# Output projection's last three tiles and the up projection's first three, in token halves

## The reference, cut to what matters

```python
def rmsnorm_2(x, g):
    y = xf * lax.rsqrt(jnp.mean(xf * xf, axis=-1, keepdims=True) + EPS)
    return (y * g.astype(jnp.float32)).astype(x.dtype)
...
    o = jnp.einsum('bhtm,bmhd->bthd', p, v).reshape(B, T, D_MODEL)
    return o @ w_o                      # cross attention's output projection
...
def conv_glu_ffn(h, w_up, conv_w, conv_b, w_down):
    u = causal_dwconv(h @ w_up, conv_w) + conv_b
    a, b = jnp.split(u, 2, axis=-1)
    return (jax.nn.silu(a) * b) @ w_down
```

## Time and profile before

| | |
|---|---|
| median of the timed runs | 2122.86 us |
| lowest, highest of three | 2119.52, 2123.41 us |
| profiled execution | 2120.05 us |
| span of its trace | 2118.2 us |
| TensorE busy | 2035.4 us (96%) |
| VectorE, ScalarE, GpSimd busy | 948.6, 892.0, 909.7 us |

### The profile page before, as it was taken

One profiled execution on the slowest core, in us unless ns is written; L12 is line 12 of the kernel. 1 busy time (PEld: TensorE's weight loads), 2 busy tenths in 40 slices (PEclk: granted clock), 3 DMA queues, 4 the chain that ended last, 5 costly groups with the idle time before them and its releaser, 6 DMA issues.

```text
span 2118.2 us, 27695 instructions
## 1 busy us (share of the span) xinstructions
PE 2035.4 (96%) x9940; PEld 1679.1 (79%) x9940; DVE 948.6 (45%) x1168; ACT 892.0 (42%) x1093; POOL 909.7 (43%) x419
## 2 busy tenths in 40 slices
PE   2999999999999999999999999999999989999998
PEld 2778877878787878888888878778798778888887
DVE  6155441454545453611112345877572257555313
ACT  2366663232323233333322346678554335444321
POOL 4422223434343433354444445759266133444443
PEclk9999999999999999999999999999999999999999
DMA  7221212433333322233233322220144122333331
GB/s 282 81 65 56 60 31 89 164 115 129 114 129 118 134 99 90 70 109 97 93 97 100 109 82 88 80 70 2 60 130 140 50 80 80 99 99 99 92 107 60
DMA packets 57390, 203.76 MB, mean 96 GB/s; under 512 B 6368, under 2 KB 8544, under 8 KB 57056
## 3 DMA queue, kind: packets, MB, share of 16 engines
q1 hardware_dynamic: 57312, 202.70, 29.9%
HBM read 200.57 MB, written 2.10 MB: 96 GB/s over the span
## 4 chain that ended last, share of the span: by engine, by line
PE 75%; issue 8%; DVE 7%; ACT 6%; POOL 4%; DMA 1%; POOLq 0%; DVEq 0%; SPq 0%; ACTq 0%
PE acc L1987 17%; PE acc L1989 17%; PE acc L1988 17%; PE aux L1987 5%; PE aux L1988 4%; PE aux L1989 4%; POOL w_lo L493 3%; ACT sp L552 2%; PE acc L2205 2%; PE aux L2465 1%; DVE qkvf L1660 1%; PE aux L2119 1%; DMA ada<-in_ada 1%; POOL cfy L516 1%; PE aux L2195 1%
## 5 line engine op out<-in xcount | busy, mean ns | idle before, releaser
L493 POOL TENSOR_TENSOR w_lo<-raw,w_hi 128x1024 fp32r<-128x1024 f32 x321 | 780.9, 2437 | 1137.4 <-ACT w_hi L552 1136.5
L552 ACT ACTIVATE w_hi<-raw 128x1024 fp32r<-128x1024 f32 x321 | 339.9, 1061 | 569.9 <-PE acc L1989 422.2
L1987 PE MATMUL acc<-x_hi,w_hi 128*128 128x512 f32 (+1 forms) x1336 | 526.2, 394 | 7.6 <-DVE x_lo L1531 4.1
L1988 PE MATMUL acc<-x_lo,w_hi 128*128 128x512 f32 (+1 forms) x1336 | 518.2, 388 | 0.0
L1989 PE MATMUL acc<-x_hi,w_lo 128*128 128x512 f32 (+1 forms) x1336 | 518.1, 388 | 0.0
L1987 PEld LDWEIGHTS acc<-x_hi,w_hi 128*128 128x128 f32 x1336 | 252.3, 189 | 64.4 <-issue 7.7
L1989 PEld LDWEIGHTS acc<-x_hi,w_lo 128*128 128x128 f32 x1336 | 252.0, 189 | 51.8
L1988 PEld LDWEIGHTS acc<-x_lo,w_hi 128*128 128x128 f32 x1336 | 252.3, 189 | 49.7 <-issue 0.5
L1165 DVE SCALAR_TENSOR_TENSOR adac<-ada,c_act,adac 128x1024 f32<-128x1024 f32 x42 | 65.7, 1565 | 98.2 <-DMA ada<-in_ada 97.3
L1432 DVE TENSOR_TENSOR ht<-acc,tn 128x512 f32<-128x512 f32 x21 | 14.5, 692 | 173.8 <-PE acc L1989 171.3
L1987 PE MATMUL aux<-w_hi,x_hi 128*128 128x512 f32 x192 | 75.9, 395 | 6.5 <-DVE x_lo L1193 5.2
(11 more groups left out here) (480 smaller groups left out, 3621.4 us busy)
## 6 DMA issues: line engine op xcount, KB each, us to landing
raw<-in_weights SPq DMA_DIRECT2D x324, 512.0 KB, 3.6
ada<-in_ada SPq DMA_DIRECT2D x48, 512.0 KB, 3.7
resid<-in_x SPq DMA_DIRECT2D x1, 2048.0 KB, 12.4
out<-resid SPq DMA_DIRECT2D x16, 128.0 KB, 1.7
decay<-in_tables SPq DMA_DIRECT2D x4, 256.0 KB, 3.6
memf<-in_mem SPq DMA_DIRECT2D x1, 1024.0 KB, 4.9
angles<-in_tables SPq DMA_DIRECT2D x1, 512.0 KB, 3.8
small<-in_small SPq DMA_DIRECT2D x1, 320.0 KB, 3.1
```

The lines of the kernel that those rows point to most:

```text
L493: nc.gpsimd.tensor_tensor(w_lo[s][:], raw[s][:], w_hi[s][:].bitcast(F32), ALU.subtract).then_inc(lo_ready, 1)
L552: return nc.scalar.activation(out, in_, func, **kw)
L1987: M(out, a_hi, b_hi, start=first, stop=False)
L1988: M(out, a_hi, b_lo, start=False, stop=False)
```

## The change

The last three tiles of the output projection (5, 6, 7) are computed in token halves: first all three over tokens 0 to 255, then all three over tokens 256 to 511. Each half has its own sum of squares, its own statistic of two products with a matrix of ones, and its own norm by Ln and Exp on ACT (`half_root`). The residual, x_hi and x_lo are made for the first half of the tokens and then for the second. The up projection's tiles 0 to 2 follow in halves; tile 3 stays in full width and goes with the second half. The second half of tile 5 has to be taken by DVE before TensorE may write tile 7's (`bank_free`). ACT's splits of up units 0 to 3, which stood right behind the tiles that gave back their buffers, now stand between the x_hi of the first half. The squares for norm 4 are made in full width beside the second half. The diff:

```diff
--- before.py
+++ after.py
@@ -361,6 +361,14 @@
             return bank(At(T0["down"] + n - 1)) if n else aux[:, 2 * T:3 * T]
 
         last_y = [down_bank(KT - 1)[:, HALVES[0]], aux[:, 0:T][:, HALVES[1]]]
+
+        xo_rs = [rs[:, HALVES[0]], aux[:, 3 * T:4 * T][:, HALVES[1]]]
+
+        def xo_half(n, h):
+
+            if h == 0:
+                return bank(At(T0["xo"] + n - 4))[:, HALVES[0]]
+            return (aux[:, 2 * T:3 * T][:, HALVES[0]], aux[:, 3 * T:4 * T][:, HALVES[0]], aux[:, 2 * T:3 * T][:, HALVES[1]])[n - 5]
 
         def up_bank(n):
 
@@ -1053,14 +1061,37 @@
             values_hi(2)
             turned(3)
             values_hi(3)
-            for n in range(1, 8):
+            for n in range(1, 5):
                 split_hi(At(U0["xo"] + n + AHEAD))
-            last_square(bank(At(T0["xo"] + 3)), U0["xo"] + 8)
-            split_hi(At(U0["up"] + AHEAD))
-            root(1.0 / D)
+
+            def half_square(h):
+                if h:
+                    act.wait_ge(unit_used, U0["xo"] + 8)
+                else:
+                    own["tile_done"].next(3)
+                own["last_sq"].own(f(sqt[:, HALVES[h]], xo_half(KT - 1, h), ACT.Square))
+
+            def half_root(h):
+                own["stat_ready"].next()
+                roots(xo_rs[h], 1.0 / D, xo_rs[h], own["rs_ready"])
+
+            def half_hi(k, c):
+                own["res_ready"].next()
+                own["norm_hi"].own(f(x_hi[:, k, c], resid[:, k, c], scale=norm_g[4][:, k:k + 1]))
+
+            half_square(0)
+            half_root(0)
+            split_hi(At(U0["up"]))
             for k in range(KT):
-                own["res_ready"].next()
-                own["norm_hi"].own(f(x_hi[:, k, :], resid[:, k, :], scale=norm_g[4][:, k:k + 1]))
+                half_hi(k, HALVES[0])
+                if k in (0, 2):
+                    split_hi(At(U0["up"] + k // 2 + 1))
+                if k == 4:
+                    half_square(1)
+                    split_hi(At(U0["up"] + 3))
+            half_root(1)
+            for k in range(KT):
+                half_hi(k, HALVES[1])
                 own["rsq_ready"].own(f(yv_o[:, k, :], resid[:, k, :], ACT.Square))
             split_hi(At(U0["up"] + 4))
             split_hi(At(U0["up"] + 5))
@@ -1523,26 +1554,52 @@
 
             def up_residual():
 
-                own["rs_ready"].next()
                 added = aux[:, 4 * T:5 * T]
 
-                def low(k):
+                def low(k, c):
                     own["norm_hi"].next()
-                    own["x_ready"].own(V.scalar_tensor_tensor(x_lo[:, k, :], resid[:, k, :], norm_g[4][:, k:k + 1],
-                                                              x_hi[:, k, :].bitcast(F32), ALU.mult, ALU.subtract))
+                    own["x_ready"].own(V.scalar_tensor_tensor(x_lo[:, k, c], resid[:, k, c], norm_g[4][:, k:k + 1],
+                                                              x_hi[:, k, c].bitcast(F32), ALU.mult, ALU.subtract))
 
                 def add_square(k):
                     own["rsq_ready"].next(2 if k == 1 else 1)
                     step.own(V.tensor_tensor(sqacc[:], sqacc[:] if k > 1 else yv_o[:, 0, :], yv_o[:, k, :], ALU.add))
 
+                def sublayer(k, h):
+                    c = HALVES[h]
+                    step.own(V.scalar_tensor_tensor(added[:, c], yv_o[:, k, c], norm_g[3][:, k:k + 1], xo_rs[h],
+                                                    ALU.mult, ALU.mult))
+                    own["res_ready"].own(V.tensor_tensor(resid[:, k, c], resid[:, k, c], added[:, c], ALU.add))
+
+                own["rs_ready"].next()
+                sublayer(0, 0)
+                half_tile(5, 1)
+                V.sem_inc(S["bank_free"], 1)
+                sublayer(1, 0)
+                low(0, HALVES[0])
+                sublayer(2, 0)
+                low(1, HALVES[0])
+                half_tile(6, 1)
+                sublayer(3, 0)
+                low(2, HALVES[0])
+                sublayer(4, 0)
+                low(3, HALVES[0])
+                sublayer(5, 0)
+                half_tile(7, 1)
+                low(4, HALVES[0])
+                sublayer(6, 0)
+                low(5, HALVES[0])
+                sublayer(7, 0)
+                low(6, HALVES[0])
+                low(7, HALVES[0])
+                own["rs_ready"].next()
                 for k in range(KT):
-                    step.own(V.scalar_tensor_tensor(added, yv_o[:, k, :], norm_g[3][:, k:k + 1], rs, ALU.mult, ALU.mult))
-                    own["res_ready"].own(V.tensor_tensor(resid[:, k, :], resid[:, k, :], added, ALU.add))
+                    sublayer(k, 1)
                     if k:
-                        low(k - 1)
+                        low(k - 1, HALVES[1])
                     if k in (3, 5, 7):
                         add_square(k // 2)
-                low(KT - 1)
+                low(KT - 1, HALVES[1])
                 for k in range(4, KT):
                     add_square(k)
                 V.sem_inc(S["sq_ready"], 1)
@@ -1889,15 +1946,34 @@
             normalize(3)
             out_low(2)
             out_low(3)
-            for n in range(KT):
-                if n < KT - 1:
+            def half_tile(n, h):
+
+                c, src = HALVES[h], xo_half(n, h)
+                if n == KT - 1:
+                    own["last_sq"].next()
+                    step.own(V.tensor_copy(yv_o[:, n, c], src))
+                    return
+                if h:
                     dve.wait_ge(unit_used, U0["xo"] + n + 1)
+                else:
+                    own["tile_done"].next()
+                step.own(V.tensor_copy(yv_o[:, n, c], src))
+                step.own(V.tensor_tensor(squares[:, c], src, yv_o[:, n, c], ALU.mult))
+                step.own(V.tensor_tensor(sqacc[:, c], sqacc[:, c], squares[:, c], ALU.add))
+                if n == KT - 2:
+                    V.sem_inc(S["sq_ready"], 1)
+                    own["sq_ready"].skip()
+
+            for n in range(5):
+                dve.wait_ge(unit_used, U0["xo"] + n + 1)
                 if n < 4:
                     sublayer_tile(n, aux[:, n * T:(n + 1) * T], yv_o[:, n, :], squares)
                 else:
-                    t = At(T0["xo"] + n - 4)
-                    sublayer_tile(n, bank(t), yv_o[:, n, :], squares, t)
-            invert()
+                    sublayer_tile(n, bank(At(T0["xo"])), yv_o[:, n, :], squares, At(T0["xo"]))
+            for n in range(5, KT):
+                half_tile(n, 0)
+                free(At(T0["xo"] + n - 4))
+            own["tile_done"].skip()
             up_residual()
 
 
@@ -2722,25 +2798,50 @@
             project(1, 6, 8)
             project(2, 4, 8)
             project(3, 4, 8)
-            for n in range(4, KT):
-                tile(At(U0["xo"] + n), At(T0["xo"] + n - 4), xo_hi, xo_lo)
-            two_part_stat()
-            spread_rs()
-
-            def up_part(n, first, end):
+            tile(At(U0["xo"] + 4), At(T0["xo"]), xo_hi, xo_lo)
+
+            def xo_stat(h):
+
+                c = HALVES[h]
+                own["sq_ready"].next()
+                M(xo_rs[h], ones, sqacc[:, c], start=True, stop=False)
+                own["last_sq"].next()
+                M(xo_rs[h], ones, sqt[:, c], start=False, stop=True).then_inc(S["stat_ready"], 1)
+
+            for h, c in enumerate(HALVES):
+                for n in range(5, KT):
+                    if h == 0:
+                        wait_bank(At(T0["xo"] + n - 4))
+                    elif n == KT - 1:
+                        own["bank_free"].next()
+                    wh, wl = weights(At(U0["xo"] + n))
+                    for k in range(KT):
+                        m = three(xo_half(n, h), wt(wh, k), wt(wl, k), xo_hi[:, k, c], xo_lo[:, k, c], k == 0, k == KT - 1)
+                        if h and n == 5 and k == 2:
+                            xo_stat(0)
+                    m.then_inc(unit_used if h else S["tile_done"], 1)
+
+            def up_part(n, first, end, c=slice(0, T)):
 
                 wh, wl = weights(At(U0["up"] + n))
                 for k in range(first, end):
-                    m = three(up_bank(n), wt(wh, k), wt(wl, k), x_hi[:, k, :], x_lo[:, k, :], k == 0, k == KT - 1)
-                if end == KT:
+                    m = three(up_bank(n)[:, c], wt(wh, k), wt(wl, k), x_hi[:, k, c], x_lo[:, k, c], k == 0, k == KT - 1)
+                if end == KT and c.stop == T:
                     m.then_inc(unit_used, 1)
 
             wait_bank(At(T0["up"]))
             wait_bank(At(T0["up"] + 1))
             for k in range(KT):
                 own["x_ready"].next()
-                for n in range(4):
-                    up_part(n, k, k + 1)
+                for n in range(3 if k >= 2 else 2):
+                    up_part(n, k if n < 2 or k > 2 else 0, k + 1, HALVES[0])
+                if k == 2:
+                    xo_stat(1)
+            for k in range(KT):
+                own["x_ready"].next()
```

(3 more changed lines are left out.)

## The result

The changed kernel takes 2127.11 us, the median of 20 runs (2122.80 to 2132.58), and the kernel before, timed beside it, 2120.86 us (20 runs, 2118.74 to 2124.61). The ratio is 1.003 with a 95% interval of [1.0024, 1.0036]: slower by 6.3 us, 5.1 to 7.6. The predicted time, 2126.0, lies near the measured one and the range holds it. The difference was forecast at +3.2, however, half of what it is, and the kernel before came out 2 us faster here than in the three runs that the forecast was set upon. It is luck that these 2 us take back most of the 3.1 by which the difference was off. The likeliest case was "within 0.2%"; the outcome is "slower".

The account below looks back on a forecast made before the run. TensorE was taken as busy nearly throughout, so only its stall and slow clock (11.3 us) could be won. The timed sum put up unit 4 at 1769.5 against 1766.30, +3.2 on 2122.86: 2126.0 us, range 2119.8 to 2129.5.

Parts of the forecast that it names:

- within 0.2%: Whole run: a difference of about 4.2 us or less, not to be told from no change; chance 0.65.
- wait for bank_free: Before tile 7's second half: TensorE stands 1.75 us until VectorE has taken tile 5's second half.
- held x_lo, beyond their work: First half on VectorE: four x_lo start inside a GpSimd w_lo, 1.9 us in all, bounds nothing and 7.1.
- second norm starts: ScalarE starts the second half's norm at 1745.6, only after the last x_hi of the first half.
- up projection's second half starts: TensorE starts the second token half of the up projection at 1751.8, after 4.0 us of standing.
- four tiles end: TensorE ends the up projection's first four tiles at 1767.1, with 1.4 us charged for the clock.
- unit 4: Up unit 4, released by its w_lo, starts at 1769.5, 3.2 us later than 1766.30.
- the half norm: Norm of each token half: table loads for Ln and Exp, 1.28 us each, make it 3.45 us instead of 0.85.
- the clock's share: Up projection's second half: TensorE's clock falls to half after idling, charged 1.4 us, bounds 0 and 1.7.
- rival (d): First half's x_lo: GpSimd holds VectorE more, two further hits at 1.78 us; +6.8 us, 2129.7; chance 0.14.
- (b): Half norms: no table load at all, the table being there already; -3.1 us, 2119.8; chance 0.06.
- (c): Half norms and first half: no table load and no x_lo held up; -5.0 us, 2117.9; chance 0.04.

Follow-up runs that it names:

- e1: Changed kernel with one preload of the table holding Ln and Exp ahead of the first half's square: 2120.68 us, ratio 0.9998 to the kernel before.
- e8: e5 with ScalarE's split of up unit 0 moved ahead of its square of tile 7: 2118.58 us, ratio 0.9984 to the kernel before.
- e3: e1 with GpSimd making only 32 of 1024 w_lo columns for up units 0 to 3, computation left out: 2117.35 us, ratio 0.998 to the kernel before.
- e4: e1 with ScalarE's split of up unit 0 ahead of the first half's square: 2121.26 us, ratio 0.9998 to the kernel before.
- e9: Changed kernel with w_lo of up units 0 to 3 in four pieces and a preload ahead of the second half's square: 2121.98 us, ratio 1.0.
- e5: e1 with each w_lo of up units 0 to 3 made in four operations of 256 columns: 2118.9 us, ratio 0.9985 to the kernel before.

## Why the prediction was half right

Point by point, with 1.2 us taken from the times of after:

| point of the forecast | forecast | measured |
|---|---|---|
| VectorE starts behind the first norm | 1728.94 | 1728.8 |
| wait for bank_free | 1.75 | 1.39 |
| tile 7's second half starts | 1731.5 | 1731.3 |
| held x_lo, beyond their work | 1.9 | 4.0 |
| second norm starts | 1745.6 | 1747.8 |
| up projection's second half starts | 1751.8 | 1753.8 |
| four tiles end | 1767.1 | 1769.4 |
| unit 4 | 1769.5 | 1771.8 |

**Right:** the half norm. The choice of two loads of 1.28 us for each norm, taken from the pair at Exp and Ln, held at both, and Ln starts 0.01 us behind its load (1726.57 + 1.28 against 1727.86), with no drain. The bank_free wait, which the changed order brings about only with the loads, came as described, and as in the sum it adds nothing itself. The stretch from the second half's start to the end of the four tiles was 15.3 in the sum and is 15.6 (1755.04 to 1770.39 + 0.23). With no slow stretch e1 takes 14.4 for the same products (1748.52 to 1762.65 + 0.23), so the clock's share is 1.2 and not 1.4, and the products take 0.5 us more than the 13.9 of the sum. (The idle time ahead of the slow stretch in the earlier trace rows is 2.4 us of 3.4, not the 2.9 that I gave.) The last 2.4 us up to unit 4 are as forecast.

**Wrong: the term for x_lo held by w_lo.** The step was "four x_lo start inside one and wait 0.1, 1.1, 0.4 and 1.1 us of remaining w_lo". The price was right, where an x_lo was hit: the end 0.28 us behind the w_lo's. The layout in time was not. I had the first x_lo meet the last 0.1 us of the first w_lo. In the trace the splits of units 0 and 1 send two w_lo one right behind the other (1731.03, 4.74 us for both), the first of them is over at about 1733.4 (2.4 us each), and x_lo starts at 1733.47: it just misses the first and is caught by the whole second. So this hit costs 2.1 us instead of almost none. The other two cost 0.9 and 1.0. A half tile takes VectorE 1.49 us with its gaps (1731.00 to 1732.49), not the 1.37 that I used. Without that error the hit would most likely have come all the same: the splits that the forecast places at 1728.9 and 1730.5 already put the second w_lo right behind the first, and in e8 an x_lo that begins 0.09 us before the end of one operation is held through the next. What was wrong is to charge the rest of the first w_lo alone. The excess of 2.1 us over my 1.9 appears again in every later point: second norm +2.2, second half +2.0, end +2.3.

This is the mechanism of rival (d), at 2.1 us beyond the forecast where it asked for 1.0 and was priced at 3.6. I gave it 0.14 although the sum's term rested on edges that I couldn't place to 0.1 us; a term with bounds of 0 and 7.1 should have carried more of the chance above its value than below.

**The rivals without loads,** as e1 and e3 let them be measured: (b) was worked out at -3.1 against the seam of before and is -0.75; 2.1 of that gap is again the held x_lo. (c), with neither loads nor held x_lo, was worked out at -5.0; e3's seam gives 46.82 - 51.58 = -4.8.

**From +5.5 to +6.3.** The medians differ by 0.8 more than the seams. In the trace of after 1.2 us lie ahead of the seam, with a slow stretch of 6.8 us near 890 us where the kernel before has one of 3.4. That does not explain them, for before has another of 3.4 near 1380 us (1377.00:1380.40 at 0.81, 1380.40:1383.80 at 0.69) where after has 1.00. Whether the change shifts the start of tile 5 or one execution differs from the next, no run tells: e1 starts tile 5 at 1714.50 and e4, with the same work up to there, at 1719.00. That share stays open.

## What to carry to other kernels

When a norm goes from one place to two halves, its fixed costs count twice: a table that ScalarE loads behind a statistic stands on the path, and one preload call ahead of the first norm took 6.3 us off the seam here (5.1 of loads, 1.2 of slow clock). The same call placed amid the first half's work cost 1.1 us there (e9), so it belongs where ScalarE is idle. When work on one engine is moved beside another's, ask whether the two share an input path: a long GpSimd operation holds each VectorE operation with two SBUF inputs that begins inside it, and cutting it in pieces bounds the hold by a piece, or by two where it begins at the end of one (the sum of 4.0 us became 16 x 0.04 = 0.6 in e5, where the 16 x_lo take 0.517 us on average). A term that depends on which of two edges comes first is to be priced at both answers, not at the one that the layout happens to give.

## What the hardware showed that I had not expected

- A VectorE operation with both inputs in SBUF does not wait for all the GpSimd work that is queued: 0.48 to 0.69 us amid 12 pieces without a gap (e5), 2.57 where the operation in flight was a whole w_lo. But one that began 0.09 us before the end of a piece was held to the end of the next (1.06 us, e8).
- GpSimd pays for short operations: 0.75 us for 256 columns (8.98 / 12) where 1024 take 2.4, so 0.6 us per unit more.
- Loads that aren't asked for come as a pair for Ln and Exp, and at each norm anew: the second norm's Ln loads again at 1749.01, so the table left by the first norm's Exp has no Ln. With one table for both loaded ahead there is none at either norm (e1). The Trainium skill, "ScalarE: Activation LUTs", section "Table sets: the hidden batching unit", counts one load for Ln and then Exp. That holds in this kernel only where that table is asked for.
